# Second attention with its meta scores taken once and two steps in flight, and five reordered places in a two-block transformer kernel

## What is computed

```python
for l in range(2):
    h = rmsnorm(x, norm_mix[l]); proj = h @ w_in[l]
    iq, ik, iw, q, k, v, hq, hf, hi, hg, ga, gb = parts of proj     # rope on q, k, iq, ik
    score = sum_h iw * relu(iq @ ik.T); keep the 128 best keys of each query
    y_attn = softmax(q @ k.T / 8, those keys) @ v
    log_f = logaddexp(log(lb), log1p(-lb) + log_sigmoid(hf)); S_t = f_t * S_{t-1} + (1 - f_t) v_t^T; o_t = S_t^T silu(hq)
    merged = sigmoid(ga) * (y_attn @ w_pa) + sigmoid(gb) * (norm(o) * silu(hg) @ w_ph)
    x = x + merged @ w_out[l];  x = x + (silu(g) * u) @ w_ffn_out[l]
```

## Time and profile before

| | us |
|---|---|
| three runs, median (lowest to highest) | 2457.68 (2456.47 to 2461.82) |
| the profiled execution, its own time | 2463.03 |
| its span, from the first to the last instruction | 2461.2 |
| PE busy | 2318.0 (94%) |
| POOL busy | 1474.4 (60%) |
| DVE busy | 1074.8 (44%) |
| ACT busy | 610.4 (25%) |
| mean granted TensorE clock | 0.974 |

### The profile page before, as it was taken

How to read it: one execution, slowest core, us unless ns; L and a number is a source line. 1 busy time by engine, 2 the same in 40 slices (tenths; PEclk the granted TensorE clock), 3 DMA queues, 4 the chain that set the end, 5 groups by cost and what they waited for, 6 DMA issues and landing times.

```text
span 2461.2 us, 30592 instructions
## 1 busy us (share of the span) xinstructions
PE 2318.0 (94%) x10971; PEld 1853.4 (75%) x10971; DVE 1074.8 (44%) x1623; ACT 610.4 (25%) x1058; POOL 1474.4 (60%) x1452
## 2 busy tenths in 40 slices
PE   5989999999999998898999999999998879999998
PEld 4666788788888886666888888888876446788887
DVE  7794772543321148847725332211382552433200
ACT  3323423321110023234233211110242551211100
POOL 5563645687677745535456866766492216776673
PEclk9999999999999998999999999999999989999999
DMA  3321223422322322212234222222331002222222
GB/s 124 118 69 52 85 72 101 154 94 96 100 94 96 101 95 92 69 52 69 82 99 156 94 102 94 94 91 97 116 112 44 1 0 69 86 95 101 94 94 77
DMA packets 68516, 217.35 MB, mean 88 GB/s; under 512 B 8256, under 2 KB 8384, under 8 KB 68288
## 3 DMA queue, kind: packets, MB, share of 16 engines
q1 hardware_dynamic: 52528, 187.72, 23.2%
q10 hardware_dynamic: 15888, 28.21, 3.2%
HBM read 195.93 MB, written 10.49 MB: 84 GB/s over the span
## 4 chain that ended last, share of the span: by engine, by line
PE 82%; DVE 12%; ACT 4%; issue 1%; DMA 1%; ACTq 0%; POOL 0%; SPq 0%; DVEq 0%; POOLq 0%
PE ps L1530 71%; PE ps L1797 2%; PE ps L1955 2%; ACT pe L937 2%; DVE score L1323 1%; DVE small L1319 1%; DVE b_sb L1380 1%; PE ps L1714 1%; DVE h_lo L1028 1%; PE ps L1747 1%; PE ps L1732 1%; DVE small L1208 1%; PE ps L1758 1%; DVE htb L1023 1%; PE ps L2012 1%
## 5 line engine op out<-in xcount | busy, mean ns | idle before, releaser
L502 POOL TENSOR_TENSOR w_lo<-w_raw,w_hi 128x512 fp32r<-128x512 f32 x700 | 955.0, 1364 | 58.4
L499 POOL TENSOR_SCALAR w_hi<-w_raw 128x512 fp32r<-128x512 f32 x700 | 497.9, 711 | 759.1 <-DMA w_raw<-wst 726.3
L1530 PE MATMUL ps<-h_hi,w_lo 128*128 128x512 f32 (+1 forms) x2048 | 807.4, 394 | 29.6 <-DVE h_lo L1028 17.3
L1530 PE MATMUL ps<-h_lo,w_hi 128*128 128x512 f32 (+1 forms) x2048 | 787.7, 385 | 0.0
L1530 PE MATMUL ps<-h_hi,w_hi 128*128 128x512 f32 (+1 forms) x2048 | 787.7, 385 | 0.0
L1530 PEld LDWEIGHTS ps<-h_hi,w_lo 128*128 128x128 f32 x2048 | 389.5, 190 | 130.8 <-issue 23.2
L1530 PEld LDWEIGHTS ps<-h_lo,w_hi 128*128 128x128 f32 x2048 | 390.5, 191 | 78.5 <-issue 6.2
L1530 PEld LDWEIGHTS ps<-h_hi,w_hi 128*128 128x128 f32 x2048 | 389.7, 190 | 76.5
L1530 PE MATMUL ps<-a_hi,w_lo 128*128 128x512 f32 (+1 forms) x572 | 214.3, 375 | 0.0
L1530 PE MATMUL ps<-a_lo,w_hi 128*128 128x512 f32 (+1 forms) x572 | 213.9, 374 | 0.0
L1530 PE MATMUL ps<-a_hi,w_hi 128*128 128x512 f32 (+1 forms) x572 | 213.8, 374 | 0.0
(11 more groups left out here) (277 smaller groups left out, 2661.2 us busy)
## 6 DMA issues: line engine op xcount, KB each, us to landing
w_raw<-wst SPq DMA_DIRECT2D x350, 512.0 KB, 3.5
rot<-raw ACTq DMA_DIRECT2D x70, 128.0 KB, 2.1
gates<-gt ACTq DMA_DIRECT2D x32, 256.0 KB, 4.1
stage<-gates ACTq DMA_DIRECT2D x32, 256.0 KB, 3.5
x_sb<-xin SPq DMA_DIRECT2D x4, 512.0 KB, 8.0
out<-x_sb SPq DMA_DIRECT2D x1, 2048.0 KB, 7.1
kc<-cst ACTq DMA_DIRECT2D x1, 1056.0 KB, 4.9
kc<-cst ACTq DMA_DIRECT2D x1, 481.0 KB, 5.0
```

The costliest lines, as they stand in the source:

```text
L499: eng.tensor_scalar(w_hi[s][:, part], w_raw[s][:, part], 1.0, 1.0, ALU.mult, ALU.mult)\
L502: eng.tensor_tensor(w_lo[s][:, part], w_raw[s][:, part], w_hi[s][:, part].bitcast(F32), ALU.subtract)\
L1530: m = eng.matmul(o, w, x, start=first and i == 0, stop=final and i == 2)
```

## The change

`LAG` becomes 3. The core of the diff, with the parts that the text speaks of:

```diff
-SCORE_BANKS = ((1, 2), (3, 7))
+SCORE_BANKS = ((3, 7), (1, 2))
+TURN_BANKS = ((1, 2), (4, 5))
...
-        def score_tile(u, i):
-            at = 0 if i == 0 else 1024 - META + 512 if u < PAIRS_A else 1024
-            return ps[:, at:at + TM]
+        def score_tile(t, i):
+            return bank(2 * (t % 2) + i)
...
-            eng.wait_ge(x_new, 16 * (LAYERS + 1))
-            eng.dma_start(out.rearrange("(k p) t -> p k t", p=P), x_sb[:, :, :]).then_inc(out_dma, 16)
+            for i in range(KT):
+                eng.wait_ge(x_new, 16 * LAYERS + KT + i + 1)
+                eng.dma_start(out[i * P:(i + 1) * P, :], x_sb[:, i, :]).then_inc(out_dma, 16)
...
@@ POOL, softmax_weights, in the steps of b
+                        if b % 2:
+                            h = (t - TB * PAIRS_A) // 2
+                            c = index[(L2, "wo2")] + h // 2
...
+                            split_half(c, c % WSLOTS, h % 2)
...
-            for n in range(2, 2 * L2 + 1, 2):
-                ahead = index[(n // 2, "ik" if n < 2 * L2 else "qa0")] + 4
+            for n in range(0, 2 * L2 + 1, 2):
+                ahead = index[(n // 2, "ik" if n < 2 * L2 else "qa0")] + (4 if n else 2)
...
@@ ACT, scans: results(3) behind the logarithms
                 eng.activation(xf[0], fl, ACT.Exp, scale=-1.0).then_inc(prep_a, 1)
-                results(PAIRS_1 - 1)
...
                 eng.activation(xf[1], xf[0], ACT.Ln, bias=small[:, 126:127]).then_inc(prep_a, 1)
+                results(PAIRS_1 - 1)
...
@@ ACT, second attention
+                eng.wait_ge(nm2_ready, t + 1)
                 for i in range(2):
-                    eng.activation(pe[u % 2][:, 2 * b + i, :], score_tile(u, i), ACT.Exp, ...
+                    eng.activation(pe[u % 2][:, 2 * b + i, at:at + T], score_tile(t, i), ACT.Exp, ...
+                eng.wait_ge(md2_ready, t + 1)
+                eng.activation(meta_cols(t), meta_cols(t), ACT.Exp).then_inc(em2_ready, 1)
...
-                eng.activation(osb2[:, :], bank(7), ACT.Copy).then_inc(y2_taken, 1)
-                eng.wait_ge(y2_taken, h + 1)
-                eng.activation(osq2[:, :], osb2[:, :], ACT.Square).then_inc(osq2_ready, 1)
+                eng.activation(osq2[:, :], bank(7), ACT.Square).then_inc(osq2_ready, 1)
...
@@ DVE: the angles' four and three instructions move out of tables() to between the additions of squares
+                    for j in range(1, 4):
                         add_square(0, j)
+                    angles()
+                    for j in range(4, KT - 1):
+                        add_square(0, j)
+                    reduced_angles()
...
@@ DVE, once, at t == 0
+            def meta_scores():
+                eng.wait_ge(mk2_ready, 1)
+                for i in range(2):
+                    eng.tensor_copy(m_sb[:, i, :], bank(6 + i)).then_inc(mk2_taken, 1)
+                eng.wait_ge(mk2_taken, 2)
+                for i in range(2):
+                    k = step(eng.tensor_reduce(nmeta[:, i:64:2], m_sb[:, i, :].rearrange("p (t m) -> p t m", m=META), AX.X, ALU.max, negate=True))
+                after(k)
             def maxima(t):
                 for i in range(2):
                     eng.wait_ge(s2_ready, 2 * t + i + 1)
+                    k = step(eng.tensor_reduce(small[:, at + i:at + i + 1], score_tile(t, i), AX.X, ALU.max, negate=True))
+                if t == 0:
+                    meta_scores()
+                after(k)
+                eng.tensor_tensor(small[:, col:col + 2], small[:, at:at + 2], nmeta[:, 2 * t:2 * t + 2], ALU.min)
+                ...
+                eng.tensor_tensor(meta_cols(t), m_sb[:, :, META * t:META * (t + 1)], less, ALU.add).then_inc(md2_ready, 1)
             def inverse_sums(t):
-                eng.wait_ge(e2_ready, 2 * t + 2)
+                eng.wait_ge(em2_ready, t + 1)
+                after(step(eng.tensor_reduce(small[:, at:at + 2], meta_cols(t), AX.X, ALU.add)))
+                after(step(eng.tensor_tensor(small[:, 16 + c:18 + c], small[:, 16 + c:18 + c], small[:, at:at + 2], ALU.add)))
                 eng.reciprocal(small[:, 32 + c:34 + c], small[:, 16 + c:18 + c]).then_inc(inv2_ready, 1)
...
@@ DVE, scans
-                step(eng.memset(af, 0.0))
                 eng.wait_ge(prep_a, 3 * l + 1)
                 eng.tensor_scalar(xf[0], xf[0], BIG, None, ALU.min).then_inc(prep_v, 1)
+                step(eng.memset(af, 0.0))
...
@@ DVE, order of a step of the second attention
             for t in range(STEPS + LAG + TB):
-                if 0 < t <= STEPS:
-                    inverse_sums(t - 1)
                 if t < STEPS:
                     maxima(t)
                 if 0 < t <= STEPS:
+                    inverse_sums(t - 1)
                     difference(t - 1)
...
@@ PE
-                    gemm_first([(l, "ik")], 0)
-                    for n in ("iq0", "iq1", "q0"):
+                    gemm_first([(l, "ik"), (l, "iq0")], 0)
+                    for n in ("iq1", "q0"):
...
-                    gemm_first([(l, n) for n in ("ik", "iq0", "iq1", "q0")], 2 * l)
+                    gemm_first([(l, n) for n in ("ik", "iq0", "iq1")], 2 * l)
+                    gemm((l, "q0"))
...
@@ PE, heads: transposes of block b
-                        if 4 * p + b:
-                            eng.wait_ge(t_taken[i], 16 * l + 4 * p + b)
+                        if b >= 2:
+                            eng.wait_ge(t_taken[i], 16 * l + 4 * p + b - 1)
+                        elif p and b == 0:
+                            eng.wait_ge(t_taken[i], 16 * l + 4 * p - 1)
                         for kb in range(b + 1):
-                            m = eng.transpose(bank(4 + i, kb * P, P), ...
+                            m = eng.transpose(bank(TURN_BANKS[b % 2][i], kb * P, P), ...
...
@@ PE, second attention: scores_2(t)
+                if t < 2:
+                    for i in range(2):
+                        taken(eng, (L2, f"vb{2 * t + i}"))
+                else:
+                    eng.wait_ge(e2_ready, 2 * t - 2)
@@ PE, once, at t == 0: 64 products of 16 columns
+            def meta_scores():
+                for t in range(STEPS):
+                    for i in range(2):
+                        m = eng.matmul(bank(6 + i, META * t, META), qab[rows, u, b * P:(b + 1) * P], kab[rows, keys_of(u), T:TM], ...)
...
+                if t == STEPS + 2:
+                    first_outputs(range(4))
...
@@ rows k = 4, 5 of wo0 to wo3; values(7) comes in the next step
+                if t == STEPS + 2:
+                    first_outputs(range(4, 6))
+            first_outputs(range(6, 7))
+            o_square_2(HH - 1)
+            first_outputs(range(7, 8))
```

More of the change, by code:

```diff
@@ L196 @@
 STEPS = TB * UNITS
-LAG = 2
+LAG = 3
 LAM_INIT = 0.8 - 0.6
@@ L497, in split @@
                 eng.sem_inc(w_seen, 1)
[L498 to L503, removed]
+                for i in range(2):
+                    split_half(c, s, i)
             def softmax_weights():
@@ L1037, in scaled_rest, with angles, reduced_angles @@
                                          ALU.mult, ALU.subtract).then_inc(h_ready, 1)
+            def angles():
+                eng.wait_ge(pos_dma, 16)
+                after(step(eng.tensor_copy(ang[:, :], posi[:, :])))
+                after(step(eng.tensor_scalar(ang[:, :], ang[:, :], inv, None, ALU.mult)))
+                magic = 1.5 * 2.0 ** 23
+                after(step(eng.tensor_scalar(kk[:, :], ang[:, :], float(1 / (2 * np.pi)), magic, ALU.mult, ALU.add)))
+                after(step(eng.tensor_scalar(kk[:, :], kk[:, :], magic, None, ALU.subtract)))
+            def reduced_angles():
+                c1 = 6.28125
+                c2 = float(np.floor((2 * np.pi - c1) * 2 ** 17) / 2 ** 17)
+                c3 = float(2 * np.pi - c1 - c2)
+                for j, c in enumerate((c1, c2, c3)):
+                    after(step(eng.scalar_tensor_tensor(rr[:, :], kk[:, :], -c, rr[:, :] if j else ang[:, :],
+                                                        ALU.mult, ALU.add)))
             def tables():
@@ L1943, in scores_2, with keys_of @@
                 u, b = divmod(t, TB)
-                if t == 0:
-                    for i in range(TB):
-                        taken(eng, (L2, f"vb{i}"))
-                eng.wait_ge(e2_ready, 2 * t) if t else None
-                keys = 0 if u < PAIRS_A else 1 + u - PAIRS_A
-                for part in (slice(0, T), slice(T, TM)):
+                if t < 2:
[3 more added lines that the diff above has]
+                    eng.wait_ge(e2_ready, 2 * t - 2)
+                for i in range(2):
+                    rows = slice(64 * i, 64 * i + 64)
+                    eng.matmul(score_tile(t, i), qab[rows, u, b * P:(b + 1) * P], kab[rows, keys_of(u), 0:T],
+                               start=True, stop=True).then_inc(s2_ready, 1)
+            def keys_of(u):
+                return 0 if u < PAIRS_A else 1 + u - PAIRS_A
+            def meta_scores():
+                taken(eng, (L2, "vbm"))
```

(21 more changed lines are left out.)

93 lines of the change are left out of this document (51 added, 42 removed).

## The result

The changed kernel took 2442.16 us (median of 4 runs, 2440.59 to 2443.79), the kernel before 2458.25 beside it: ratio 0.9933, 95% interval 0.9916 to 0.995. That is 16 us less; forecast were 48, to 2409.7, with a range up to 2427. The direction was right, the size a third. The profiled execution took 2443.28 us, span 2441.4, so 19.8 under the profiled one of before.

A forecast was written before the change was run, and what follows sets the result against it. PE was taken as the bound, mostly full-rate products, so only its waits could be won: 12.4 + 9.9 + 12.5 + 5.7 + 4.5 + 3.0 = 48.0 us off 2457.7 gave 2409.7, range 2393 to 2427.

The forecast's parts named there:

- 1. First products and tables: Layer 0's start: two outputs first and tables moved into DVE's waits bring index scores earlier; 12.4 us won, 5.5 to 14.
- sine comes at 37.3 + 3 + 6.8: Layer 0 tables: norm ends at 37.3, small instructions take 3, angles 6.8; sine at 47.1 in place of 59.67.
- what follows is a fixed order: Layer 0 after the sine: copies, `q1`, `q2` follow unchanged, so index scores move from 75.15 by the same 12.5 us.
- 2. Layer 1: Layer 1's start, three outputs instead of four: index scores 9.9 us earlier, low 3, high 11.
- 3 and 4. Heads and scans: Two pairs of banks for the heads' transposes win 12.5 us; scans' logarithms no longer behind a copy win 5.7.
- 5. Second attention: From first scores to wo's first result: 178 us against 182, 4.5 won; low -8, high +20.
- a step with values ... 6.65: Second attention, unit of `a`: values 4.6 us, then ACT's copy, DVE's subtraction and copy; 6.65 us, making the unit 15.5.
- my signs of being wrong: Large DVE idle time in `b`, turning transfers still landing 9 to 10 us late, or attention's granted clock below 0.8.
- 6. Store: End of kernel: only the last eighth stands behind the last tile; 3.0 us won, low 2, high 5.
- Attention loses 8: Rival, second attention: DVE's small instructions and POOL's open 0.95 us outweigh the second tile; 2422 us, chance 0.12.
- the starts give one product each: Rival, both layers' starts: only 5.5 us each, transfers stay at 9.8, POOL's splitting slows tables; 2421, chance 0.10.
- The lower clock through all of attention: Rival, second attention: PE stays at its lower clock, 1.2 GHz, making the kernel slower; 2479 us, chance 0.02.

The follow-up runs named there:

- tables_late: Changed kernel with the gate's 13 small DVE instructions and ACT's three moved from layer 0's tables to its scans: 2430.89 us, ratio 0.9882 to the kernel before.
- five_only: Changed kernel with the second attention, first wo rows and POOL's early halves put back as before: 2421.92 us, ratio 0.984 to the kernel before.
- ahead: Changed kernel with the next step's scores on PE and maxima on DVE put before a unit's values: 2425.81 us, ratio 0.9862 to the kernel before.
- heads_only: Kernel before with only the heads' transposes in two pairs of banks, both layers: 2449.65 us, ratio 0.9957.
- inv_first: Changed kernel with DVE's inverse sums of step t-1 put back before the maxima of step t: 2449.51 us, ratio 0.9954 to the kernel before.
- meta_twice: Changed kernel with the 64 meta products done twice at the same place: 2452.07 us, ratio 0.9969 to the kernel before.

## Why the prediction was wrong

**1. First products and tables: failed by 7.** The norm went as worked out. The step that failed is "sine comes at 37.3 + 3 + 6.8": the 3 for the small instructions, my own estimate, measured 8.2, and the sine came 4.8 late. I had read that DVE takes 1.49 instead of 0.42 beside POOL and used it only where POOL's work was removed, not where it went. tables_late shows it. The other 2.3 us failed in "what follows is a fixed order": behind PE's wait of 5.4 the 48 products up to the index scores took 14.0 at a granted clock of 0.82, where before they took 11.6 at 1.00. In tables_late, where that wait is 1.1, the clock is 1.00. The low end of 5.5 was the right number for another reason.

**2. Layer 1.** Right: 9.8 against 9.9, PE's wait 2.2 (forecast 1 to 2). That it fits so well is in part luck. Two errors of 1.3 cancel: the turning transfers landed 8.7 us behind the copy of `ik` (896.95 - 888.25), not 7.4, and `ik` was whole 8.9 earlier (19.8 less the 10.9 won before), not 7.6. And five_only and ahead, with the same code up to there, began these scores at 900.92 and 901.2, 7 earlier than the changed kernel (907.99).

**3 and 4. Heads and scans.** 14.7 in the table's second and fourth rows against 18.2. heads_only gives 10.6 for the first, so 4 are left for the scans, both under the forecast and inside their bounds; DVE's wait in layer 1 left PE 5.0, not 3.5. The pairs are 19.3 us apart, 20.8 before, as the term needs. The waits give 1.1 of these 1.5; the 0.15 a pair that I added for semaphores is read from no row, and what the other 0.4 is was not measured.

**5. Second attention: failed by 19.** Forecast 178 from the first scores to wo's first result, measured 194.3 (2048.27 - 1853.96). In the prediction's own terms: start 31.9 for 30; the three `a` units 52.8 (17.0, 17.0, 18.8) for 46.5; three `b` units 69.4 for 62.5; tail 40.2 for 38.7. The step that failed is "a step with values ... 6.65". I let DVE's maxima and small instructions (2.3 us) lie beside PE's values, while the values began only 1.2 after those maxima did, behind ACT's copy of the meta rows (1.24 in the row of `a`), and the next scores stood behind the values: 8.0. In `b` the block is 7.3 at a granted clock of 0.64, not 6.1, and DVE stands 5.3 waiting for the scores behind it. I had summed one engine (DVE) where a ring over two engines decided; ahead, which cuts that ring, gives the forecast 15.5 for two of three units of `a`, and 17.9, 21.4 and 20.9 for the 19, 22 and 22 of `b`. How much of a `b` unit is the lower clock and how much the ring alone, no run separates. The start was seen (meta 10, measured 9.4) but not weighed: it eats all that the second tile gains.
These 16.3 are not yet the 19.4 of the table: 0.9 is my rounding of 181.6 - 178 up to 4.5, and from wo's first result to the long chain it took 39.1 instead of 36.9.

POOL's latency was sized right (0.92 for 0.95), but it was not what binds: inv_first took it away and lost 5. Of my signs of being wrong, two came: DVE's idle time in `b` stayed large (busy 14.25 of 24.00), and the granted clock there was 0.78. My low end of -8 for this term was the range's mistake; it held costs that I could name and no order of work between engines.

**6. Store.** 5.1 for 3.0, at the high end. The 4.1 that I took is of transfers beside others; the last 256 KB alone landed in 2.4. The Trainium skill's 2.6 ("DMA: Bandwidth & Descriptors", section "Anatomy of one DMA — SWDGE (gpsimd) path"), a fit for transfers that GpSimd issues where these come from SP, is near that, and was the better estimate.

**The rivals.** "Attention loses 8" had the right place and sign at half the size; "the starts give one product each" came true for layer 0 alone, and its reason, POOL's splitting beside the tables, was the right one. Either rival would still have been 20 us under the measured time: the two came together, and the attention lost more than its low end. The lower clock through all of attention did not come: 1.00 in `a`, 0.78 in `b`, and 0.88 from the first scores to wo's first result, where it was 0.89 before.

## What to carry to other kernels

Where two engines wait for each other once a unit, find the instruction that each puts in front of what the other needs next; a serial sum over the busier one is a lower bound, not the period. Work that is held back to clear one stretch must be charged to the stretch it moves into, most of all to tiny instructions there. And hoisting small products out of a loop puts them bare at its front if nothing else can run: 9.4 us here, where per step they lay inside a 1.26 us block.

## What the runs showed of the hardware that was not expected

An instruction of 128x4 elements takes 0.16 us, and up to 1.25 beside POOL's splitting; one of 128x528 (L1272) 0.77 and 1.10. The meta products kept PE busy without a gap, and yet the granted clock fell. In the changed kernel it was 1.00 in the 10.9 us of dense products in front of them and 0.76 from 1855 to 1864. Length, busy times and clock in meta_twice:
```profile
1850.00:1862.00 12.00, 12.00 (x144) 12.00 (x144) 1.06 (x2) 0.00 (x0) 0.00 (x0) 0.64 0.14 43
1862.00:1873.00 11.00, 11.00 (x106) 11.00 (x106) 0.00 (x0) 0.00 (x0) 0.00 (x0) 0.50 0.00 0
```
The second half of them ran at 1.2 GHz, so doubling them cost 14.5 us and not 9.4. In layer 0, the first products behind PE's wait of 5.4 us were 0.43 us apart, where the same kind stood 0.23 apart in front of it.
